# A slot's gate weights are loaded once its gate products are done, not once its up products are

## The reference

```python
def expert_chunk(args):
    xc, e = args
    return (jax.nn.silu(xc @ w_g[e]) * (xc @ w_u[e])) @ w_d[e]
```

## Time and profile before

| | us |
|---|---|
| median of 3 runs | 1726.19 |
| lowest, highest | 1723.5, 1726.23 |
| the profiled execution | 1724.38 |
| its span, first to last instruction | 1722.5 |
| expert loop, first gate product to last down product | 1077.1 to 1661.7 |
| mean granted clock of TensorE, share of full speed | 0.91 |

### The profile page before, as it was taken

The page is one execution under the profiler, slowest core; times in us unless marked ns, Lnnn a source line. Parts: engine busy times, 40 slices in busy tenths (PEclk is TensorE's granted clock), DMA queues, the critical chain, the costliest instruction groups (busy, mean ns, idle before and its releaser), DMA issues. The chain is left out here.

```text
span 1722.5 us, 22851 instructions
## 1 busy us (share of the span) xinstructions
PE 1418.5 (82%) x7480; PEld 830.2 (48%) x7480; DVE 680.9 (40%) x1314; ACT 371.5 (22%) x796; POOL 196.1 (11%) x348
## 2 busy tenths in 40 slices
PE   5999999478889888823599942999999999999950
PEld 4665445378656556511355521445444544454420
DVE  3497787501488777645122255001000100010008
ACT  4000111330366554430111100111111111111103
POOL 0000011362100000014000000011111111111111
PEclk8999999788589999966699975999999999999985
DMA  7500000474330000045311107699999999999917
GB/s 267 231 1 6 13 16 19 154 240 123 111 99 14 2 1 2 1 141 146 152 61 61 41 17 302 258 393 401 405 412 386 409 400 402 377 396 395 396 50 291
DMA packets 83021, 326.79 MB, mean 190 GB/s; under 512 B 12319, under 2 KB 48288, under 8 KB 64834
## 3 DMA queue, kind: packets, MB, share of 16 engines
q1 hardware_dynamic: 65130, 287.76, 42.7%
q0 software_dynamic: 15440, 37.09, 6.4%
q10 hardware_dynamic: 2384, 1.06, 0.2%
HBM read 311.20 MB, written 29.45 MB: 198 GB/s over the span
## 5 line engine op out<-in xcount | busy, mean ns | idle before, releaser
L1792 PE MATMUL ps<-arena 128*128 128x512 f32 x544 | 239.9, 597 | 0.0
L1792 PEld LDWEIGHTS ps<-arena 128*128 128x128 f32 x544 | 102.1, 190 | 136.9 <-issue 136.8
L521 DVE SCALAR_TENSOR_TENSOR arena<-arena 128x1024 f32<-128x1024 f32 x120 | 147.5, 1282 | 1.2
L1489 PE MATMUL ps<-arena 128*128 128x512 f32 (+1 forms) x288 | 129.6, 603 | 15.3 <-DVE arena L1584 15.3
L354 PE MATMUL ps<-arena 128*128 128x512 f32 (+1 forms) x384 | 141.2, 527 | 0.0
L1800 PE MATMUL ps<-arena 128*64 128x256 f32 x1088 | 121.2, 380 | 0.0
L308 PE MATMUL ps<-arena 128*128 128x352 f32 x384 | 117.5, 467 | 4.3 <-issue 3.9
L1844 PE MATMUL ps<-arena 128*128 128x512 f32 x272 | 119.6, 591 | 0.0
L1090 ACT ACTIVATE arena<-ps,arena 128x640 f32<-128x640 f32 (+7 forms) x128 | 89.9, 703 | 108.9 <-DVE arena L1167 101.9
L354 PEld LDWEIGHTS ps<-arena 128*128 128x128 f32 x384 | 72.0, 189 | 67.2 <-issue 61.6
L999 PE MATMUL ps<-arena 128*128 128x128 f32 x528 | 87.3, 289 | 20.4 <-DVE arena L1185 9.8
(11 more groups left out here) (365 smaller groups left out, 1549.7 us busy)
## 6 DMA issues: line engine op xcount, KB each, us to landing
arena<-in_w_gate SPq DMA_DIRECT2D x34, 2048.0 KB, 9.8
arena<-in_w_up SPq DMA_DIRECT2D x34, 2048.0 KB, 14.3
arena<-in_w_down SPq DMA_DIRECT2D x34, 2048.0 KB, 13.8
arena<-in_x_prompt SPq DMA_DIRECT2D x16, 512.0 KB, 6.5
arena<-in_cache_cmp SPq DMA_DIRECT2D x64, 128.0 KB, 2.8
arena<-in_cache_cmp POOLq DMA_DIRECT2D x64, 128.0 KB, 2.9
arena<-in_cache_sel SPq DMA_DIRECT2D x64, 128.0 KB, 2.1
arena<-scratch_y SPq DMA_DIRECT2D x16, 512.0 KB, 5.8
```

What stands on the lines that cost most here:

```text
L521: ins = dve.scalar_tensor_tensor(o, i, dw[:, c, j:j + 1], o, ALU.mult, ALU.add)
L1489: mm = pe.matmul(ps[:n, 2 + half, :], mixT[:, t % 2, k, 0:n], w_out[:, k, 512 * half:512 * half + 512], start=(k == 0), stop=(k == KT_ - 1))
L1792: mm = pe.matmul(ps[:, bank, :], xgT_l[:, k, :], w[LARGE][:, k, :], start=(k == 0), stop=(k == KT_ - 1))
```

## The change

SP no longer waits once per slot, for the up products, ahead of both loads. It waits for the slot's gate products ahead of the gate load, and for its up products ahead of the up load. PE's two signals after the gate products are renamed `gated0` and `gated1` and raised by one at the start of the block, and ACT's waits for them are one higher. The order of loads on SP's queue, and all that is computed, stay.

```diff
@@ expert_weights
                     for s, e in enumerate(places):
-                        sp.wait_ge(sem(f"upped{s}"), i + 1)
-                        for w, name in ((w_gate, "w_gate"), (w_up, "w_up")):
+                        for w, name, used in ((w_gate, "w_gate", "gated"), (w_up, "w_up", "upped")):
+                            sp.wait_ge(sem(f"{used}{s}"), i + 1)
                             sp.dma_start(w[s], a[name][bass.ds(e, 1)].rearrange("a (p k) n -> (a p) k n", k=KT_))\
                               .then_inc(sem(f"{name}_in{s}"), 16)
@@ expert_products
                     pe.wait_ge(sem("w_gate_in0"), i * 16 + 16)
-                    project_large(w_gate, 0).then_inc(sem("gated_l"), 1)
+                    project_large(w_gate, 0).then_inc(sem("gated0"), 1)
...
                     pe.wait_ge(sem("w_gate_in1"), i * 16 + 16)
-                    project_small(w_gate, 2).then_inc(sem("gated_s"), 1)
+                    project_small(w_gate, 2).then_inc(sem("gated1"), 1)
@@ expert_silu
-                    act.wait_ge(sem("gated_l"), i + 1)
+                    act.wait_ge(sem("gated0"), i + 2)
                     act.activation(hid_l, ps[:, 0, :], ACT.Silu).then_inc(sem("silu_l"), 1)
-                    act.wait_ge(sem("gated_s"), i + 1)
+                    act.wait_ge(sem("gated1"), i + 2)
                     act.activation(hid_s, ps[:, 2, 0:HH], ACT.Silu).then_inc(sem("silu_s"), 1)
@@ block of the expert stage, PE
-                for name in ("upped0", "upped1", "downed0", "downed1", "xg_turned0", "xg_turned1"):
+                for name in ("gated0", "gated1", "upped0", "upped1", "downed0", "downed1", "xg_turned0", "xg_turned1"):
                     pe.sem_inc(sem(name), 1)
```

## The result

| | before | after |
|---|---|---|
| median, us | 1724.63 (10 runs) | 1742.52 (10 runs) |
| lowest, highest, us | 1722.64, 1727.28 | 1733.07, 1752.86 |
| ratio to before, 95% interval | 1 | 1.0104, 1.0077 to 1.0132 |
| the profiled execution, its span, us | 1724.38, 1722.5 | 1743.65, 1741.7 |

The change makes the kernel about 18 us slower, 1.04%. It also makes it restless: ten runs of before lie within 4.6 us, ten of after within 20.

What follows compares the result with a forecast made beforehand. PE was taken to bound the expert loop, busy throughout rounds 1 to 16. Terms of 0 + 0 + 0 + 0 + 0 left the profiled 1724.38 at 1724.4; the middle of four times, 1725.3 us, was predicted, range 1721.5 to 1730.

Steps and rivals of the forecast that it cites:

- What bounds the kernel: Expert loop, rounds 1 to 16: PE busy 548.86 of 548.86 us, 34.30 us a round, so PE sets the time.
- the weights' lead: Gate loads land before their readers start: 11.8 us early for the large slot, 15.9 us for the small.
- All five parts costed at nothing: Large gate load, small gate load, up and down loads, SP's queue, semaphores: each 0 us on PE.
- The moved issue: Large slot's gate load: issued 6.9 us earlier, landing 3.3 us earlier, worth 0 us on PE.
- What the earlier load collides with: POOL's small gather beside the earlier gate load: grows by about 1 us, 0 us on PE.
- limit of 10.46 us: Time the small gather may take from its issue to PE's wait ahead of the down products; it took 5.2.
- the gather of 1193.5: Small gather taking 6.1 us, claimed to be in a round in which the loads left no hole.
- The Trainium skill's turns: DMA engines alternate queues by packet, so a second weight load takes no further turn from POOL's queue; gather growth stays limited.
- The slower rival: Small gather arrives last at 12.2 us, PE waits 1.7 us before the down products each round: 1753 us, chance 4%.
- The faster rivals: Gate groups' heads hide a wait for weights: 1708 us, 1%; or the loop is bound by transfers: 1672 us, 1%.

Runs made afterwards that it cites:

- the small-slot run: Changed kernel, but only the small slot's gate load waits for its gate products; the large slot's waits for its up products as before: 1724.96 us, ratio 1.0000.
- the gather-first run: Changed kernel's loads, but POOL issues the gathers for the round after next behind the large scatter, ahead of the small scatter: 1727.45 us, ratio 1.0013.

## Why the prediction was wrong

*What bounds the kernel.* Right. PE bound the loop before, and the weights' lead was real: no run shows PE waiting for weights in rounds 1 to 16. All five parts costed at nothing by this argument stand: both gate loads' own landings, the up and down loads, SP's added waits (the small-slot run has one of them, the gather-first run both, and both have rounds of 34.30 us), and the semaphores.

*The moved issue.* Right: 7.3 us into the round, landing after 11.1 us, forecast 11 to 13; the lead of the weights grew by some 4 us, and was worth nothing.

*What the earlier load collides with.* This is the step that failed. Its chain, its reader and its limit of 10.46 us were right. The growth of the gather was put at 1 us, with 7.2 us as the upper bound of its time, and so the term on PE at 0. The gathers grew by 5 us in the median (the small one by 6.4), to 14.0 us at most, and the term on PE was 19.5 us. The bound came from a gather "in a round in which the loads left no hole", at 1193.5, and that was a misreading: a hole is there in every middle round of before, some 13 to 15 us into it, and the slowest gather met it too. Around the gather of 1193.5 it looks like this, from 1195 to 1197:

```profile
q0 software_dynamic: 150, 0.48, 83.9%
q1 hardware_dynamic: 7, 0.07, 16.2%
```

Nothing in the trace before showed a gather beside a full queue for its whole way. The nearest row that did show an indirect transfer so placed was in my own groups: the large scatter is issued at 1281.72, and what waits for its landing starts at 1291.94. It takes 9.2 us, with as many rows as the large gather and beside packets of 8 KB, and is near what the gathers came to. With 9 to 10 us instead of 7.2, the small gather's margin would have been 0.5 to 1.5 us and not 3.3, and the rival close to an even chance. I used that scatter only to argue against the rival ("ran beside full loads already"), where it was the price.

*The Trainium skill's turns*, page "DMA: Bandwidth & Descriptors", section "Queues, rings and completion order". The rule that an engine takes turns by packets was cited to make the rival less likely. The runs agree with turns, and the rule argues the other way: by it a row of a gather pays for the weight packet beside it, and splitting the loads into smaller packets did take the loss away (1.0003 against 1.0104). I had tied it to 6.1 and 7.2 us, which were not measured beside a full queue.

*The slower rival.* It named the mechanism, the engine, the wait and the place, and its small gather of 12.2 us is what the late rounds show (10.4 to 14.0). That PE would stand in every round was wrong. Its size was 28 us, worked out as 1.7 us in each of 16 rounds; measured are 19.5 us in 8 rounds, of which 15.3 us are lateness of the down products (22.7 to 25.6 us into a round) and the rest is slower products. The chance of 4% was the larger error, not the size.

*The faster rivals.* Neither shows: PE has no wait for weights that could be given back, and the kernels without the loss and with POOL's old order are at 1724 to 1725, as before.

## What to carry to other kernels

A gap in a load queue is not spare time until one has asked what else uses it: look at the traffic by queue inside it, not at the DMA share as a whole. Price a small transfer beside a full queue only by one that ran beside a full queue for its whole way, a scatter if there is no gather, and look at the size of the packets beside it; and where its reader has less margin than that price, moving an unrelated load forward is a risk, even if the loaded data have all the lead in the world. Cheap cures were smaller packets of the large loads, a later start of the next load, or an earlier issue of the small transfer; here none of them beats the kernel before, since PE fills the round.

## What the hardware did that I had not expected

The packet size of one queue goes with the slowest transfers of another. With the same bytes, and gate and up packets of 16, 8 and 4 KB for the large slot, the gathers had a maximum of 14.0, 10.7 and 9.6 us, and medians of 10.1, 9.5 and 7.6. This is one profiled execution each, and those with split loads happened to be the fastest of their twelve.

A short wait can cost more than itself. In the round shown, PE stood for 2.24 us and its next 16 products took 8.83 us instead of 7.03. By stretch (PEclk is the third number from the end):

```profile
1384.60:1386.60 2.00, 2.00 (x4) 1.00 (x5) 0.00 (x0) 0.00 (x0) 0.00 (x0) 0.74 1.08 459
1386.60:1388.20 1.60, 1.60 (x3) 0.57 (x3) 0.00 (x0) 0.00 (x0) 0.00 (x0) 0.50 0.92 389
1388.20:1390.00 1.80, 1.80 (x5) 0.80 (x4) 0.00 (x0) 0.00 (x0) 0.00 (x0) 0.78 1.03 437
```

The granted clock fell to 0.50, the 1.2 GHz level, after that wait and came back within some 4 us. This happened in 2 of the 8 rounds with a wait; the other one had waited 1.43 us. Two rounds with waits of 2.28 and 2.33 us kept the full clock, so the length of the wait alone does not decide. It adds 3.6 of the 19.5 us. Part of the wide scatter of the runs may come from it: the three slowest of the ten executions, 1749 to 1753 us, had the lowest mean clock (0.902 to 0.904, the others 0.906 to 0.911). That fits, but nothing was run to test it.
